# Grouped differential-attention heads: weights in thirds, squares with their sums, and a new order of VectorE's steps in a head

## What is computed

```python
h = rms_norm(x, attn_norm[0])
q, k = apply_rope(rms_norm(q, q_norm)), apply_rope(rms_norm(k, k_norm))   # per head, 2 x 64 columns each
p = softmax(q @ k.T / sqrt(64), causal)                                   # two maps per head
a = p[0] - lam * p[1]
o = rms_norm(a @ v, subln) * (1.0 - lambda_init)                          # 128 columns per head
x = x + o.reshape(B, S, 1024) @ w_o
```

## Time and profile before

| | us |
|---|---|
| three runs, median | 2990.15 |
| lowest, highest | 2986.58, 2995.16 |
| the profiled execution | 2997.06 |
| its span, first to last instruction | 2995.2 |
| TensorE busy in it | 2789.4 (93%) |
| VectorE busy | 1825.8 (61%) |
| ScalarE busy | 1081.1 (36%) |
| GpSimd busy | 131.6 (4%) |

### The profile page before, as it was taken

The page is one execution under the profiler, slowest core; times in us unless marked ns, Lnnn a source line. Parts: engine busy times, 40 slices in busy tenths (PEclk is TensorE's granted clock), DMA queues, the critical chain, the costliest instruction groups (busy, mean ns, idle before and its releaser), DMA issues.

```text
span 2995.2 us, 40999 instructions
## 1 busy us (share of the span) xinstructions
PE 2789.4 (93%) x14220; PEld 2338.0 (78%) x14220; DVE 1825.8 (61%) x2871; ACT 1081.1 (36%) x1778; POOL 131.6 (4%) x166
## 2 busy tenths in 40 slices
PE   7999899999787999998986899999998998899998
PEld 6777688887776788887875788888888887788886
DVE  6767567675665567767996554354455555464545
ACT  5444332323664322223112232132233566352432
POOL 4111000000110000000000000000000000000000
PEclk8999899999999999998997999999998999999999
DMA  3111245452101355542110121112111000232221
GB/s 111 64 56 43 85 162 188 163 178 97 43 29 50 113 182 176 176 147 67 54 50 28 50 71 63 57 64 67 59 37 71 15 29 15 64 98 94 96 90 65
DMA packets 69313, 252.07 MB, mean 84 GB/s; under 512 B 7840, under 2 KB 10144, under 8 KB 66592
## 3 DMA queue, kind: packets, MB, share of 16 engines
q1 hardware_dynamic: 69152, 249.99, 24.7%
HBM read 247.87 MB, written 2.10 MB: 83 GB/s over the span
## 4 chain that ended last, share of the span: by engine, by line
PE 62%; DVE 16%; issue 15%; ACT 4%; DVEq 2%; POOLq 1%; POOL 0%; ACTq 0%; DMA 0%; SPq 0%
PE psum L1869 16%; PE psum L1870 16%; PE psum L1871 16%; DVE work L1397 4%; PE psum L2257 2%; DVE w_lo L1226 1%; ACT work L1028 1%; PE psum L2009 1%; ACT sw_pt L1040 1%; PE psum L1987 1%; PE psum L2246 1%; PE psum L1988 1%; PE psum L1989 1%; DVE w_lo L1593 1%; DVE tok_ms L1516 1%
## 5 line engine op out<-in xcount | busy, mean ns | idle before, releaser
L1869 PE MATMUL psum<-hx_hi,w_hi 128*128 128x512 f32 x1568 | 626.6, 400 | 28.1 <-DVE w_lo L1226 12.8
L1871 PE MATMUL psum<-hx_hi,w_lo 128*128 128x512 f32 x1568 | 624.0, 398 | 0.0
L1870 PE MATMUL psum<-hx_lo,w_hi 128*128 128x512 f32 x1568 | 622.6, 397 | 0.0
L710 ACT ACTIVATE w_hi<-w_raw 128x1024 fp32r<-128x1024 f32 (+1 forms) x328 | 344.8, 1051 | 528.6 <-PE psum L1871 227.3
L1226 DVE TENSOR_TENSOR w_lo<-w_raw,w_hi 128x1024 fp32r<-128x1024 f32 (+1 forms) x328 | 398.3, 1214 | 180.5 <-ACT w_hi L710 162.0
L1869 PEld LDWEIGHTS psum<-hx_hi,w_hi 128*128 128x128 f32 x1568 | 296.7, 189 | 79.0 <-issue 16.7
L1871 PEld LDWEIGHTS psum<-hx_hi,w_lo 128*128 128x128 f32 x1568 | 297.0, 189 | 74.0
L1870 PEld LDWEIGHTS psum<-hx_lo,w_hi 128*128 128x128 f32 x1568 | 297.3, 190 | 48.4
L1869 PE MATMUL psum<-a_hi,w_hi 128*128 128x512 f32 (+1 forms) x656 | 235.9, 360 | 19.7 <-DVE a_lo L1338 10.8
L1871 PE MATMUL psum<-a_hi,w_lo 128*128 128x512 f32 (+1 forms) x656 | 234.0, 357 | 0.0
L1870 PE MATMUL psum<-a_lo,w_hi 128*128 128x512 f32 (+1 forms) x656 | 233.5, 356 | 0.0
(11 more groups left out here) (300 smaller groups left out, 4905.9 us busy)
## 6 DMA issues: line engine op xcount, KB each, us to landing
mod_w<-in_w_mod SPq DMA_DIRECT2D x96, 512.0 KB, 3.6
w_raw<-in_fup SPq DMA_DIRECT2D x88, 512.0 KB, 4.5
w_raw<-in_cup SPq DMA_DIRECT2D x88, 512.0 KB, 3.4
w_raw<-in_fdown SPq DMA_DIRECT2D x32, 512.0 KB, 4.6
w_raw<-in_cdown SPq DMA_DIRECT2D x32, 512.0 KB, 3.5
w_raw<-in_da_qkv SPq DMA_DIRECT2D x6, 1536.0 KB, 6.5
w_raw<-in_fdown SPq DMA_DIRECT2D x16, 384.0 KB, 3.1
w_raw<-in_cdown SPq DMA_DIRECT2D x16, 384.0 KB, 3.0
```

What stands on the lines that cost most here:

```text
L710: r = act.activation(w_hi[:, off:off + n], w_raw[:, raw:raw + n], ACT.Copy)
L1869: pe.matmul(dst, wh, xh, start=first, stop=False)
L1870: pe.matmul(dst, wh, xl, start=False, stop=False)
L1871: return pe.matmul(dst, wl, xh, start=False, stop=last)
```

## The change

- **Loads in thirds.** Blocks 2 to 7 come as three transfers of 512 KB, each with a semaphore of its own. Thirds 0 and 1 are asked for when VectorE has made the low part of the same third of the block before (`wlo`), third 2 when the whole block before is complete.
- **Where thirds are split.** In heads 1 to 5 thirds 0 and 1 are split in slot 0 and third 2 in slot 3, on both engines. In head 0 it stays at one third in each of slots 1 to 3. ScalarE does it behind `outputs_high`, VectorE behind `combine`.
- **VectorE's order.** `output_norm` comes behind the rotation, `outputs_low` directly behind the rotation and ahead of `combine`.
- **Means.** The squares of q and k are written 65 columns apart, with HD * EPS in the 65th, and a plain sum is the mean times 64; the factor goes into the gains. The outputs' squares are made by four instructions with a sum each on ScalarE, GpSimd adds P * EPS ahead of its root, and the factor goes into `sub_gain`. `output_means` is gone.
- **Reciprocals.** One of two columns for two of one.

```diff
@@ loads, on SyncE's queue
-                    with sp.Fori(2, nb) as i:
-                        load(st, 0, i, i + b0)
+                    def load_part(bi, part):
+                        cols = slice(D * part, D * (part + 1))
+                        sp.dma_start(w_raw[:, cols], dram[st["w"]][bi, :, cols]).then_inc(s_loaded[part], 16)
+
+                    sp.wait_ge(s_lo, b0 + 2)
+                    for part in range(3):
+                        load_part(2, part)
+                    with sp.Fori(3, nb) as i:
+                        for part in range(2):
+                            sp.wait_ge(s_da["wlo"], 2 * i + (part - 5))
+                            load_part(i, part)
+                        sp.wait_ge(s_lo, i + b0)
+                        load_part(i, 2)
@@ order of the splits
+        FIRST_REFILL, REFILL = ((), (0,), (1,), (2,)), ((0, 1), (), (), (2,))
@@ GpSimd
+            def root_of_sum(a, b, ready, value, done):
+                pool.wait_ge(ready, value)
+                pool.tensor_tensor(tok_ms[:, a:b], tok_ms[:, a:b], out_eps[:], ALU.add)
+                pool.drain()
+                pool.tensor_tensor(tok_r[:, a:b], tok_ms[:, a:b], half[:, a:b], ALU.pow).then_inc(done, 1)
+
             def angles():
+                pool.memset(head_sq[:, :, :, HD:HD + 1], HD * EPS)
+                pool.memset(out_eps[:], P * EPS)
                 pool.wait_ge(s_small, 32)
...
-                                root(16, 20, s_da["oms"], h + 1, s_da["por"])
+                                root_of_sum(16, 20, s_da["osq"], h + 1, s_da["por"])
@@ ScalarE
-                    act.activation(work[:, 2048 + 256 * (t % 2):2304 + 256 * (t % 2)], pb[:, bank, 0:256], ACT.Square,
-                                   scale=root)
+                    act.activation(head_sq[:, t % 2, :, 0:HD], pb[:, bank, 0:256].rearrange("p (n f) -> p n f", n=4),
+                                   ACT.Square, scale=root)
...
-                    act.activation(da_osq[:], da_osb[:].rearrange("p t e -> p (t e)"), ACT.Square)\
-                       .then_inc(S["osq"], 1)
+                    for t in range(4):
+                        r = act.activation(da_osq[:, t * P:(t + 1) * P], da_osb[:, t, :], ACT.Square,
+                                           accum_out=tok_ms[:, 16 + t:17 + t])
+                    r.then_inc(S["osq"], 1)
...
-                    if i and new:
-                        refill(h, par, i - 1)
                     if i == 3 and not first:
                         outputs_high(h - 1)
+                    if new:
+                        for part in (FIRST_REFILL if first else REFILL)[i]:
+                            refill(h, par, part)
@@ VectorE
-                    mean_squares(work[:, 2048 + 256 * (t % 2):2304 + 256 * (t % 2)].rearrange("p (n f) -> p n f", n=4),
-                                 8 + 4 * (t % 2), 4, HD, S["rms"])
+                    dve.tensor_reduce(tok_ms[:, 8 + 4 * (t % 2):12 + 4 * (t % 2)],
+                                      head_sq[:, t % 2], AX, ALU.add).then_inc(S["rms"], 1)
...
-                    dve.reciprocal(ratio[:, i:i + 1], row_sum[:, 2 * i + 1:2 * i + 2])
-                    dve.reciprocal(inv0[:, 4 * par + i:4 * par + i + 1], row_sum[:, 2 * i:2 * i + 1])
+                    dve.reciprocal(inv0[:, par, i, :], row_sum[:, 2 * i:2 * i + 2])
...
-                    if i == 2 and not first:
-                        output_norm(h - 1)
                     if i == 0:
                         rope(j + 3, 3)
                     elif more:
                         rope(j + 3, i - 1)
-                    combine(h, par, i)
-                    if i == 1 and not first:
-                        output_means(h - 1)
-                    if i and new:
-                        refill(h, par, i - 1)
+                    if i == 2 and not first:
+                        output_norm(h - 1)
                     if i == 3 and not first:
                         outputs_low(h - 1)
+                    combine(h, par, i)
+                    if new:
+                        for part in (FIRST_REFILL if first else REFILL)[i]:
+                            refill(h, par, part)
```

More of the change, by code:

```diff
@@ L67, in add @@
             loads[0] += blocks
+            loads[1] += blocks - 2
+            loads[2] += blocks - 2
         elif kind in ("kv", "q"):
@@ L208, in program @@
         neg_max = sbuf("neg_max", [P, 16])
-        inv0 = sbuf("inv0", [P, 8])
+        inv0 = sbuf("inv0", [P, 2, 4, 2])
+        out_eps = sbuf("out_eps", [P, 4])
         ratio = sbuf("ratio", [P, 4])
@@ L258, in program @@
         g4, g4_neg = work[:, 3072:3328], mag
+        head_sq = sw_vb[:, :, 0:4 * (HD + 1)].rearrange("p a (n f) -> p a n f", n=4)
         _, sw_va = layout(("va_gap", [P, 12 * D], F32), ("sw_va", [P, 2, 4 * D], F32))
@@ L314, in program @@
                  "pje", "qte", "ex", "ate", "osq", "ohi",
-                 "rms", "rope", "mx", "comb", "osb", "oms", "osc", "olo",
-                 "pr", "por", "whi")
+                 "rms", "rope", "mx", "comb", "osb", "osc", "olo",
+                 "pr", "por", "whi", "wlo")
         s_da = {k: sem(f"da_{k}") for k in names}
@@ L560, in head_gains @@
                 gains_qk = rows("da_qk_norm")
-                pool.tensor_scalar(g4[:, 0:128], gains_qk[:, 0:128], HD ** -0.5, None, ALU.mult)
-                pool.tensor_copy(g4[:, 128:256], gains_qk[:, 128:256])
+                pool.tensor_scalar(g4[:, 0:128], gains_qk[:, 0:128], 1.0, None, ALU.mult)
+                pool.tensor_scalar(g4[:, 128:256], gains_qk[:, 128:256], HD ** 0.5, None, ALU.mult)
                 pool.drain()
@@ L619, in _ @@
                             if t == 1:
-                                root(16, 20, s_da["oms"], h + 1, s_da["por"])
+                                root_of_sum(16, 20, s_da["osq"], h + 1, s_da["por"])
                     root(12, 16, s_da["rms"], 32, s_da["pr"])
-                    root(16, 20, s_da["oms"], 7, s_da["por"])
-                    root(16, 20, s_da["oms"], 8, s_da["por"])
+                    root_of_sum(16, 20, s_da["osq"], 7, s_da["por"])
+                    root_of_sum(16, 20, s_da["osq"], 8, s_da["por"])
                     rope_gains()
@@ L644, in widen @@
                         pool.wait_ge(S["inv"], m + 1)
-                        pool.tensor_copy(inv_wide[:], inv0[:, 0:4].unsqueeze(2).broadcast_to([P, 4, HD])).then_inc(S["invw"], 1)
+                        pool.tensor_copy(inv_wide[:], inv0[:, 0, 0:2, :].rearrange("p a c -> p (a c)").unsqueeze(2).broadcast_to([P, 4, HD])).then_inc(S["invw"], 1)
                     for m in range(-2, 17):
@@ L896, in output_squares @@
                     act.wait_ge(S["osb"], h + 1)
-                    act.activation(da_osq[:], da_osb[:].rearrange("p t e -> p (t e)"), ACT.Square)\
-                       .then_inc(S["osq"], 1)
+                    for t in range(4):
+                        r = act.activation(da_osq[:, t * P:(t + 1) * P], da_osb[:, t, :], ACT.Square,
+                                           accum_out=tok_ms[:, 16 + t:17 + t])
+                    r.then_inc(S["osq"], 1)
                 def refill(h, par, part):
+                    act.wait_ge(s_loaded[part], 16 * (h + (st["loads0"][part] + (1 if part else 3))))
                     if part == 0:
-                        act.wait_ge(s_loaded[0], 16 * (h + (st["loads0"][0] + 3)))
                         act.wait_ge(s_mm, h + (st["block0"] + 1))
@@ L1555, in combine @@
                     dve.wait_ge(S["ex"], 8 * h + (2 * i + 2))
-                    dve.reciprocal(ratio[:, i:i + 1], row_sum[:, 2 * i + 1:2 * i + 2])
-                    dve.reciprocal(inv0[:, 4 * par + i:4 * par + i + 1], row_sum[:, 2 * i:2 * i + 1])
+                    dve.reciprocal(inv0[:, par, i, :], row_sum[:, 2 * i:2 * i + 2])
                     dve.drain()
-                    dve.scalar_tensor_tensor(ratio[:, i:i + 1], ratio[:, i:i + 1], row_sum[:, 2 * i:2 * i + 1],
+                    dve.scalar_tensor_tensor(ratio[:, i:i + 1], inv0[:, par, i, 1:2], row_sum[:, 2 * i:2 * i + 1],
                                              neg_lam[:], ALU.mult, ALU.mult)
@@ L1567, in outputs @@
                     dve.tensor_tensor(da_osb[:], pb[:, 7, :].rearrange("p (t e) -> p t e", t=4),
-                                      bc(inv0[:, 4 * par:4 * par + 4], P), ALU.mult).then_inc(S["osb"], 1)
+                                      bc(inv0[:, par, :, 0], P), ALU.mult).then_inc(S["osb"], 1)
                     dve.drain()
-                def output_means(h):
-                    dve.wait_ge(S["osq"], h + 1)
-                    mean_squares(da_osq[:].rearrange("p (t e) -> p t e", t=4), 16, 4, P, S["oms"])
                 def output_norm(h):
@@ L1594, in refill @@
                                           ALU.subtract)
-                    if part == 2:
-                        r.then_inc(s_lo, 1)
+                    r.then_inc(s_lo if part == 2 else S["wlo"], 1)
```

(5 more changed lines are left out.)

## The result

The changed kernel takes 2973.12 us (median of five runs, 2964.70 to 2973.38), 0.9938 of before (95% interval 0.9927 to 0.9950): faster, by 17 us where 26 were forecast. The profiled execution took 2973.38, its span 2971.6. The predicted range of 2957 to 2980 holds it; the forecast of 2964 is 9 us too low.

A forecast was written before the change was run, and what follows sets the result against it. TensorE and VectorE take turns being late, neither full, with waits and lower clock. Six heads save 28.4, head 0 0.6, the end gives back 2.3: net 26.7, 2997.06 to 2970, less 7 to the median: 2964; range 2957 to 2980.

The forecast's parts named there:

- What bounds the heads: Heads 1 to 6: TensorE and VectorE late by turns; without waits, at full clock, 28.8 us a head against 33.9.
- VectorE's slack and the places of it: Heads: VectorE's work falls from 28.3 to 25.7 us, slack 3.1; 0.3 a head allowed for slot 1's later rotation.
- head 6's splits: Head 6, slots 1 and 2: two splits of the next weights wait for ScalarE, costing 0.4 us.
- VectorE as the bound: Rival, heads: slot 1's maxima late by 1 us more each head, six heads lose 6: 2970; chance 0.15.
- The clock came back: Rival, heads: waits go but 2.8 us a head at the lower clock stay: 2980; chance 0.10.
- The slower case: Rival, slot 3: ScalarE's late high part delays the low part and work behind it; 3005 at 7 late; chance 0.05.
- The loads: SyncE's queue: eighteen loads of 512 KB, three in a row at most 20 us against a head of 29; covered.
- Head 0 and the start: Head 0: TensorE's waits for its first two rotations shrink 0.3 us each, 0.6 saved.
- The end: Head 7's slot 3: low part delays the last combination; 2.3 us lost with squares, up to 1.3 more at lower clock.
- The squares: End of the heads' stage: four ScalarE squares with sums and GpSimd's addition cost 0.4 us more before the root.
- From the profiled execution to the median: Whole kernel: net 26.7 off the profiled 2997.06 gives 2970; 7 more off, as the median lies below: about 2964.
- Everything behind it shifts as a block.: Stages behind the heads: the change touches only some 280 us of 2995; the rest moves unchanged, at no cost.

The follow-up runs named there:

- placed: Changed kernel with its two new small tiles kept in free columns of sw_vb, so no other tile moves: 2964.78 us, ratio 0.9912.
- the pad: Changed kernel with three unused 128x256 products on VectorE at the end of slot 0, heads 1 to 5: 2975.69 us, ratio 0.9963.
- before again: Kernel before the change, unedited, run again on another chip day: 2989.23 us, ratio 1.0001.
- after again: Changed kernel, unedited, run again: 2973.52 us, ratio 0.9937 to the kernel before.
- Both padded kernels: Changed kernel with three unused VectorE products at the end of slot 0, or of slot 1, heads 1 to 5: 2975.69 and 2971.16 us.

## Why the prediction was right, and where it was not

**What bounds the heads.** Right, and the number in part by luck. Without waits and at clock 1.00 a head takes 28.78, for 28.8 forecast. But with the tiles in their old places head 1 takes 28.47 (placed):

```profile
75.63:104.10 28.47, 28.47 (x163) 24.02 (x162) 20.83 (x47) 16.42 (x50) 5.82 (x6) 1.00 0.19 56
```

Its slots are 6.87, 6.30, 7.06 and 8.25, where the prediction had 6.91, 6.30, 7.2 and 8.4. Slots 2 and 3 were set 0.15 too high each, and the moved tiles, which had no term, brought 0.3 back.

**VectorE's slack and the places of it.** Right, on the safe side. I had slot 1's rotation end 0.3 later than before and allowed 0.3 a head for it. It ended 0.5 sooner: in head 2 it ends 5.3 us behind the slot's first scores (110.35 to 115.67), in before 5.8 (119.40 to 125.20). The maxima start 0.3 later but are done as early, since the second map's no longer wait for scores, and from the sum of the squares to the rotation's first product it is 0.34 (113.41 to 113.75) for 0.76 (122.47 to 123.23), 0.4 less and not 0.3. So the splits in slot 0 cost nothing, and some 0.8 was left there, as the pad shows. The 0.4 for head 6's splits was about right (29.15 from its first scores to head 7's). So 173.05 for 175.0, and 171.28 with the tiles in their old places.

**The rivals.** VectorE as the bound didn't happen, but was near: another 0.8 us in slot 0 is where it begins. The clock came back wholly. The slower case needed ScalarE's high part to be late: VectorE stood 0.22 us ahead of the low part in slot 3, and that by its own issue.

**The loads.** As expected; the eighteen transfers land in 3.6 us (median), and nothing waits for them.

**Head 0 and the start.** Head 1 begins at 74.62 for 76.65, 2.0 us sooner and not 0.6. Of that 0.6 is in head 0, as forecast (28.57 for 29.19 from its first scores to head 1's), and 1.4 ahead of it. One pair of profiles can size neither: before again has 30.37 in head 0, and its first scores at 45.81 where before has them at 47.46.

**The end.** The mechanism was right: 2.3 predicted, and up to 1.3 on top if the clock drops; 3.2 measured in after, where it dropped, and 1.7 in placed, where it didn't. TensorE waited 1.86 for the combination where it had waited 0.17, for the low part, in before; that is 1.7 (1.9 predicted). The lower clock cost 1.1 in six projection matmuls and 0.5 in the values. The prediction's 1.3 was a slip: 3 us at 0.38 a us are 1.1. That it stood beside the sum as a condition was right, since three of the seven profiles with this wait show the drop. The squares, sized at 0.4, cost nothing: four stand 0.29 to 0.31 us apart, not 0.36 as in the earlier trace rows, the addition with its drain takes 0.35, and from the first square to the root it is 1.70 us for 1.67. The Trainium skill (ScalarE: Activation LUTs, What ACT_TABLE_LOAD costs) gave an estimate of 0.9 us for the four without the reading of the sums; the rows have 1.18 from the first start (275.78) to the last end (276.67 and 0.29), between that and my 1.45.

**From the profiled execution to the median.** Here the step failed that cost most. 26.7 off the profiled execution of 2997.06 is 2970.4; I then took off 7 more, by which that execution lay above its median. The profiled execution of after took 2973.38 and its median is 2973.12: there was nothing to take off. Some 4 of the 7 were in the six heads of before's profile (203.4, where the two other profiles with before's instructions have 199.1 and 199.5), so the saving had them already and they were subtracted twice. Where the other 3 were no run shows.

**"Everything behind it shifts as a block."** This is the other step that failed. I read the diff's new tiles as storage without a price. The tail of after is 5.4 us longer than before's, and the pace of its matmuls makes 4.9 of that. Against placed, after again is 7.5 to 8.7 us slower (by ratios and by medians): 4.9 by that pace, 1.8 in the six heads (173.06 and 171.28), and 1.5 at the end (34.3 and 32.77), where no run shows the address to be the cause.

Together, one profile against the other: 2970.4 forecast for the profiled execution, minus 2.0 in the six heads, minus 1.4 ahead of head 0, plus 0.9 at the end, plus 5.4 in the tail, plus 0.1 between these two is 2973.4, and 2973.38 was measured. So apart from the 7 the terms are 3 us off in sum, and that is little because they partly cancel.

## What to carry to other kernels

Slack is read place by place: 1.6 us on VectorE were free at the end of slot 1 and cost 0.8 at the end of slot 0, with the same sum of idle time. And a stretch of one profiled execution that shows the lower clock is itself a sample: take its saving from several profiles, or don't subtract the excess over the median again.

## What the runs showed of the hardware beyond that

In the feed-forward stages the starts of 512-column matmuls at clock 1.00 depend on where the tiles stand: 233.3 ns apart with before's addresses and 128 bytes above them, 234.3 ns with 64 bytes. In the mixers' stage it isn't so plain. Both padded kernels, with after's addresses and only VectorE's instructions in the heads changed, took 570.7 and 570.8 us from root to root where all others took 577.4 to 577.9. Their matmuls start 229.6 ns apart there, for 234.0 with before's addresses, 234.1 to 234.2 with 64 bytes and 232.1 with 128. So something beside the address has a part in it; what that is stayed open.
